# Two transformer-like blocks in one kernel: the memory's keys and values move into the MLP's last quarter, and the second block starts by token halves

## The reference, cut to what matters

```python
# end of the first block: an MLP of width 4096, then a norm over the features
h = rms_norm(x, g_mlp)
f = square(relu(h @ w_1))                       # 1024 -> 4096
x = x + f @ w_2                                 # 4096 -> 1024
x = rms_norm(x, g_final)

# second block (inputs with the suffix _2)
h = rmsnorm(x, norm_g)                          # norm of a norm: only factors per token
qk_raw, v, o, z_a, gates, u, z_b, qc, z_c = split(h @ w_in)
ig, fg = gates + b_gates                        # 4 heads each: they feed exponentials and cumulated sums over time
y_b = (pool(u) @ pool_w) * scale * silu(z_b)    # causal running means of 2, 4, 8, 16 tokens
km, vm = split(rmsnorm(mem, mem_norm_g) @ w_kv) # 256 memory rows, 4 heads
y_c = (softmax(q_c @ km.T / sqrt(128)) @ vm) * silu(z_c)
y_a = mlstm(qk_raw, v, o, ig, log_sigmoid(fg)) * silu(z_a)
x = x + concat(y_a, y_b, y_c) @ w_out           # y_b's part: blocks "ob"; y_c's: "oc"; y_a's: "oa"
out = rmsnorm(x, final_norm_g)
```

## Time and profile before

| | us |
|---|---|
| median of 3 runs | 2609.71 (2609.51 to 2610.11) |
| the profiled execution | 2607.73 |
| its span | 2605.9 |
| TensorE matmul busy | 2486.5 (95%) |
| VectorE busy | 1348.3 (52%) |
| ScalarE busy | 823.8 (32%) |
| mean granted TensorE clock | 0.982 |
| mean DMA rate | 54 GB/s |

### The profile page before, as it was taken

The page is one execution under the profiler, slowest core; times in us unless marked ns, Lnnn a source line. Parts: engine busy times, 40 slices in busy tenths (PEclk is TensorE's granted clock), DMA queues, the critical chain, the costliest instruction groups (busy, mean ns, idle before and its releaser), DMA issues.

```text
span 2605.9 us, 26395 instructions
## 1 busy us (share of the span) xinstructions
PE 2486.5 (95%) x11144; PEld 2011.0 (77%) x11144; DVE 1348.3 (52%) x1832; ACT 823.8 (32%) x1224; POOL 2.8 (0%) x7
## 2 busy tenths in 40 slices
PE   7999999999999999999999999998789999999678
PEld 6778677686786788888888888887678777878577
DVE  5588697897782724342232332334665333631365
ACT  5352432526113622331131220322422231221354
POOL 0000000000000000000000000000000000000000
PEclk9999999999999999999999999999899999999889
DMA  4102012021210112211111111121112111111401
GB/s 136 45 21 74 25 59 68 12 83 39 91 49 26 34 55 77 77 49 49 49 49 49 49 49 49 49 65 41 42 52 58 33 33 49 48 49 54 125 20 62
DMA packets 226680, 139.45 MB, mean 54 GB/s; under 512 B 12922, under 2 KB 221050, under 8 KB 226562
## 3 DMA queue, kind: packets, MB, share of 16 engines
q1 hardware_dynamic: 226562, 137.76, 17.9%
HBM read 128.27 MB, written 9.47 MB: 53 GB/s over the span
## 4 chain that ended last, share of the span: by engine, by line
PE 82%; DVE 11%; ACT 5%; issue 1%; DMA 1%; SPq 1%; DVEq 0%; ACTq 0%
PE bank L572 25%; PE bank L574 25%; PE bank L573 25%; PE bank L636 2%; PE bank L606 1%; DVE evens L1620 1%; DVE lru L1584 1%; DVE both L1633 1%; DVE odds L1627 1%; PE bank L821 1%; PE bank L837 1%; PE bank L729 1%; DVE wlo L1479 0%; DVE v L1558 0%; DVE lru L1574 0%
## 5 line engine op out<-in xcount | busy, mean ns | idle before, releaser
L572 PE MATMUL bank<-h_hi,whi 128*128 128x512 f32 x2000 | 788.1, 394 | 7.6 <-DVE wlo L1479 4.0
L574 PE MATMUL bank<-h_hi,wlo 128*128 128x512 f32 x2000 | 780.0, 390 | 0.0
L573 PE MATMUL bank<-h_lo,whi 128*128 128x512 f32 x2000 | 779.7, 390 | 0.0
L572 PEld LDWEIGHTS bank<-h_hi,whi 128*128 128x128 f32 x2000 | 376.5, 188 | 90.3 <-issue 11.3
L573 PEld LDWEIGHTS bank<-h_lo,whi 128*128 128x128 f32 x2000 | 376.5, 188 | 81.1 <-issue 3.6
L574 PEld LDWEIGHTS bank<-h_hi,wlo 128*128 128x128 f32 x2000 | 376.3, 188 | 79.1
L954 ACT ACTIVATE whi<-raw 128x1024 fp32r<-128x1024 f32 (+2 forms) x212 | 216.6, 1023 | 474.6 <-PE bank L574 469.3
L1479 DVE TENSOR_TENSOR wlo<-raw,whi 128x1024 fp32r<-128x1024 f32 (+2 forms) x212 | 251.1, 1185 | 208.9 <-ACT whi L954 207.4
L574 PE MATMUL bank<-ff_hi,wlo 128*128 128x512 f32 x512 | 199.2, 389 | 0.0
L572 PE MATMUL bank<-ff_hi,whi 128*128 128x512 f32 x512 | 199.2, 389 | 0.0
L573 PE MATMUL bank<-ff_lo,whi 128*128 128x512 f32 x512 | 199.2, 389 | 0.0
(11 more groups left out here) (354 smaller groups left out, 3142.7 us busy)
## 6 DMA issues: line engine op xcount, KB each, us to landing
raw<-in_w_in SPq DMA_DIRECT2D x92, 512.0 KB, 3.7
raw<-in_w SPq DMA_DIRECT2D x64, 512.0 KB, 3.8
raw<-in_w_b_out SPq DMA_DIRECT2D x16, 384.0 KB, 3.1
raw<-in_w_out SPq DMA_DIRECT2D x11, 512.0 KB, 3.5
x_in<-in_x SPq DMA_DIRECT2D x8, 512.0 KB, 5.6
raw<-in_w_a_out SPq DMA_DIRECT2D x8, 512.0 KB, 4.1
raw<-in_w_o SPq DMA_DIRECT2D x8, 512.0 KB, 3.6
xcols<-in_x SPq DMA_DIRECT2D x16, 256.0 KB, 2.8
```

The lines of the kernel that those rows point to most:

```text
L572: pe.matmul(target, lh, rh, start=start, stop=False, skip_group_check=True)
L573: pe.matmul(target, lh, rl, start=False, stop=False, skip_group_check=True)
L574: last = pe.matmul(target, ll, rh, start=False, stop=stop and point is not None, skip_group_check=True)
```

## The change

**The list of weights and TensorE's order.** Key blocks 0 and 1 go before `w2` block 5, and all other key and value blocks before `w2` block 6 of the last quarter. The memory is turned in two parts, behind `w2` blocks 2 and 3. Blocks 6 and 7 of `w2` come last, both first halves of tokens before the second ones. The token sums, the factors, their spreading and `h3` are made for each half of the tokens: the sums of the first half behind the first half of block 7 and the second half of block 6, its spread factors in the middle of block 7's second half. `gates` and `u` 0 run together, tile by tile of h3 (`tiles_together`), for the first half, with the sums of the second half in their middle; then the second half's factors, `u` 1's first half, `gates` and `u` 0 together for the second half, `u` 1's second half. Then `zb` and `pw` of group g with `u` of g+2 behind. The turn of `x_row` and the spreads `y1_scale` stand behind the last `pw`.

**DVE and ACT.** `x1`'s squares and sums go in halves of 512 tokens. `h3_low` subtracts one tile behind `h3_part`'s product. The row chain of the gates is cut: sums behind group 0, maxima (`gate_maxima`) behind the `ob` additions. The residual is scaled in front of the `ob` additions. In group g the steps of `pooled` for the next groups stand behind `yp_tile(g)`.

**SP.** The table `rcnt` is loaded with the memory. SP's wait for `m_row` stands behind the weight loads up to the second `qc` block, no longer behind those near the gates.

**Memory.** `row`, `tmp2` and `sqm` get other places.

```diff
--- before
+++ after
+        KV_AT = {5: (0, 1), 6: tuple(range(2, 2 * NH))}
...
             for j in range(DT):
                 need(("w1", f, j), w_1, 0, DT, (f * DT + j) * P, P)
             for j in range(DT):
+                if f == FC - 1:
+                    for c in KV_AT.get(j, ()):
+                        need_kv(c)
                 need(("w2", f, j), w_2, f * D, DT, j * P, P)
-        for c in range(NH):
-            need(("kv", c), w_kv, 0, DT, c * P, P)
...
+        for g in range(NH + 1):
+            if g < NH:
+                need(("u", g), w_in2, 0, DT, Y_U + g * P, P)
+            if g:
+                need(("zb", g - 1), w_in2, 0, DT, Y_ZB + (g - 1) * P, P)
+                need(("pw", g - 1), A["pool_w_2"][0, g - 1], 0, 1, 0, P)
...
+            sp.dma_start(rcnt[:], A["rcnt"]).then_inc(*landed("rcnt", ("rcnt",)))
...
-            ahead(number["gates"] + 2)
+            ahead(number["qc", 0] + 1)
             w.wait_ge(*at("m_row"))
...
+            def stat_sums(half):
+                w.wait_ge(*at("square_sums", DT - 1, half))
                 for n in range(2):
-                    for t in range(NT):
+                    for t in range(half * 4, half * 4 + 4):
                         last = pe.matmul(stat_bank[:, n * NT + t:n * NT + t + 1], square_sum[n][:, t * P:(t + 1) * P], ones[:, 0:1],
                                          start=True, stop=True, skip_group_check=True)
...
+                for j in range(DT if f < FC - 1 else DT - 2):
+                    if f == FC - 1:
+                        for c in KV_AT.get(j, ()):
+                            key_block(c)
+                    block(("w2", f, j), ff, f"ff{f}")
+                    if f == FC - 1 and j in (2, 3):
+                        turn_memory(4 * j - 8)
+                        turn_memory(4 * j - 6)
+            for c in range(2, NH):
+                key_block(c)
+            value_banks = [bank("values", q) for q in range(NM)]
+            for c in range(NH, 2 * NH):
+                value_block(c, value_banks)
+
+
+            for j in (DT - 2, DT - 1):
+                block_product(number["w2", FC - 1, j], ("w2", FC - 1, j, 0), ff, f"ff{FC - 1}", 0, used=False)
+            block_product(number["w2", FC - 1, DT - 2], ("w2", FC - 1, DT - 2, 1), ff, f"ff{FC - 1}", 1)
+            stat_sums(0)
+
+            def tiles_together(keys, half, right, right_name, middle=None):
+                together = [bank(*key, half) for key in keys]
+                for n in range(DT):
+                    if middle and n == 4:
+                        middle()
+                    w.wait_ge(*at(f"{right_name}_lo", n, half))
+                    for key, b in zip(keys, together):
+                        k = number[key]
+                        hi, lo = weight_views(k)
+                        w.wait_ge(*at("w", k))
+                        point = [(*key, half)] + ([("used", k)] if half else []) if n == DT - 1 else None
+                        three_products(b[:], (hi[:, n, :], lo[:, n, :]), (right[0][n][:, cut(half)], right[1][n][:, cut(half)]), n == 0,
+                                       point)
+
+            def factors(column, half, name):
+                w.wait_ge(*at("r12", half))
+                spread(column, half, name)
+
+            tiles_together([("w2", FC - 1, DT - 1)], 1, ff, f"ff{FC - 1}", lambda: factors(8, 0, "h3_scale"))
+
+
+            tiles_together([("gates",), ("u", 0)], 0, h3, "h3", lambda: stat_sums(1))
+            ring.names, ring.turn = ring.names + [("x1_var", 0), ("stat", 1)], 6
+            factors(8, 1, "h3_scale")
+            block_product(number["u", 1], ("u", 1, 0), h3, "h3", 0, used=False)
+            tiles_together([("gates",), ("u", 0)], 1, h3, "h3")
+            block_product(number["u", 1], ("u", 1, 1), h3, "h3", 1)
...
+            for g in range(NH):
+                block(("zb", g), h3, "h3")
+                pool_product(g)
+                if g + 2 < NH:
+                    block(("u", g + 2), h3, "h3")
+            b = bank("x_turn")
+            w.wait_ge(*at("x_row"))
+            for c in range(NT):
+                last = pe.transpose(b[:, c * NH:(c + 1) * NH], row[0][0:NH, c * P:(c + 1) * P], ident[0:NH, 0:NH])
+            last.then_inc(*up("pe_done", ("x_turned",)))
+            for half in range(2):
+                spread(0, half, "y1_scale")
...
+            columns = lambda n, half: slice(8 * n + 4 * half, 8 * n + 4 * half + 4)
+            for j in (DT - 2, DT - 1):
+                stat_square(j, 0)
+            root(columns(0, 0), "r1_0")
+            root(columns(1, 0), "r2_0")
+            ahead(number["w2", FC - 1, DT - 2] + 3)
+            stat_square(DT - 2, 1)
+            h3_part(0, 0, 1, 2)
+            stat_square(DT - 1, 1)
+            ahead(number["w2", FC - 1, DT - 1] + 3)
+            h3_part(0, 3, 4, 5)
+            root(columns(0, 1), "r1_1")
+            h3_part(0, 6)
+            root(columns(1, 1), "r2_1")
+            h3_part(0, 7)
...
+            gate_rows(0)
+            u_tile(0, 0)
+            h3_part(1, *range(DT))
+            gate_rows(1)
+            u_tile(0, 1)
+            ahead(number["zb", 0])
+            ahead(number["pw", 0])
+            split_pooled(0)
+            u_tile(1, 0)
+            u_tile(1, 1)
+            ahead(number["u", 2])
+            for g in range(NH):
+                zb_tile(g)
+                if g + 1 < NH:
+                    ahead(number["zb", g + 1])
+                split_yp(g)
+                if g < 2:
+                    split_pooled(g + 1)
+                    u_tile(g + 2, 0)
+                    u_tile(g + 2, 1)
+                ahead(number["u", g + 3] if g + 3 < NH else number["zb", NH - 1] if g == 1 else number["ob", min(g - 2, 1)])
+                if g == 0:
+                    act.activation(R(2), row[1][32:32 + NH, :], ACT.Copy).then_inc(*did(("f_row",)))
+                    w.wait_ge(*at("f_min"))
+                    act.activation(R(3), R(3), ACT.Exp).then_inc(*did(("f_exp",)))
+                    w.wait_ge(*now("act_done"))
+                    act.activation(R(3), R(3), ACT.Ln, bias=1.0).then_inc(*did(("f_ln",)))
+                if g == 1:
+                    split_pooled(3)
...
+            def square_sums(j, half):
+                total, weighted, sq_ = square_sum[0][:, cut(half)], square_sum[1][:, cut(half)], sqm[(2 * j + half) % 4]
+                w.wait_ge(*at("sqm", j, half))
                 own()
                 if j:
-                    dve.tensor_tensor(square_sum[0][:], square_sum[0][:], sqm[j % 2][:], ALU.add).then_inc(*did())
-                    dve.scalar_tensor_tensor(square_sum[1][:], sqm[j % 2][:], GF2[:, j, 1:2], square_sum[1][:], ALU.mult,
-                                             ALU.add).then_inc(*did(("square_sums", j)))
+                    dve.tensor_tensor(total, total, sq_[:], ALU.add).then_inc(*did())
+                    dve.scalar_tensor_tensor(weighted, sq_[:], GF2[:, j, 1:2], weighted, ALU.mult, ALU.add).then_inc(
+                        *did(("square_sums", j, half)))
...
+            for j in (DT - 2, DT - 1):
+                x2_tile(FC - 1, j, 0)
+                square_sums(j, 0)
+            w.wait_ge(*at("kv", 2 * NH - 1))
+            for n in range(3):
+                dve.memset(uw[n][:, 0:PAD_U], 0.0).then_inc(*did(*([("u_clear",)] if n == 2 else [])))
+            x2_tile(FC - 1, DT - 2, 1)
+            means(0)
+            second_means(0)
+            factors(0)
+            ahead(number["w2", FC - 1, DT - 2] + 3)
+            h3_part(0, 0, 1)
+            square_sums(DT - 2, 1)
+            h3_part(0, 2)
+            x2_tile(FC - 1, DT - 1, 1)
+            h3_low()
+            square_sums(DT - 1, 1)
+            ahead(number["w2", FC - 1, DT - 1] + 3)
+            h3_part(0, 3, 4, 5)
+            means(1)
+            h3_part(0, 6)
+            second_means(1)
+            h3_part(0, 7)
+            factors(1)
+            h3_low()
+            h3_part(1, *range(DT))
+            h3_low()
...
+            ahead(number["zb", 0])
+            ahead(number["pw", 0])
+            pooled(0)
+            ahead(number["u", 2])
+            for g in range(NH):
+                zb_tile(g)
+                if g + 1 < NH:
+                    ahead(number["zb", g + 1])
+                yp_tile(g)
+                if g < 2:
+                    pooled(g + 1)
+                ahead(number["u", g + 3] if g + 3 < NH else number["zb", NH - 1] if g == 1 else number["ob", min(g - 2, 1)])
+                if g == 0:
+                    gate_sums()
+                if g == 1:
+                    pooled(3)
+            w.wait_ge(*at("x_turned"))
+            dve.tensor_copy(xcol[:], bank("x_turn")[:, 0:NH * NT]).then_inc(*did(("xcol",), ("free", "x_turn")))
+            for half in range(2):
+                b = bank("y1_scale", half)
+                w.wait_ge(*at("y1_scale", half))
+                for j in range(DT):
```

(3 more changed lines are left out.)

404 lines of the change are left out of this document (193 added, 211 removed).

## The result

| | before | changed | 
|---|---|---|
| median of the runs | 2609.89 (2609.51 to 2610.11) | 2572.81 (2571.66 to 2573.80) |
| the profiled execution | 2607.73 | 2573.80 |
| its span | 2605.9 | 2571.8 |
| mean granted TensorE clock | 0.982 | 0.984 |

The changed kernel is faster: the ratio is 0.9858, with a 95% interval of 0.9841 to 0.9875. I had 2579.1 with 2571 to 2590.

The account below looks back on a forecast made before the run. TensorE, busy 95% of the span, bounds the kernel; only its waits and slow stretches count. 266.7 + 0.5 + 7.1 + 3.5 + 2.7 + 1.0 = 281.5 against 312.1, 30.6 less, gives 2579.1, range 2571 to 2590.

Parts of the forecast that it names:

- Work, 266.7: TensorE's work from 1715.9 to 2028.0, counted at the full clock: 266.7 us of a stretch of 312.1.
- The weight of `w2` 6, 0.5: Behind six short key and value blocks in a row, only this weight comes late, by 0.5 (bounds 0 and 4.4).
- The factors of the first half: DVE and ACT's 2.15 is covered by 2.7 of `w2` 7's second half; the wait of 3.9 goes.
- h3's first half, 7.1: Beside `gates` and `u` 0, TensorE waits for DVE's low parts: 7.1 in all, bounds 0 and 13.1.
- Low clock there, 3.5, and 1.0 behind `pw` 3: Clock falls once in h3's first half, costing 3.5 (bounds 0 and 9); 1.0 more behind the last pooling product's wait.
- The weight of `pw` 3, 2.7: Split behind pooled tile 3 and group 2's gating, it comes 2.7 late for TensorE (bounds 0 and 6).
- The rows, the pools and the scaling: Waits of 8.3 for `x_row` and 2.8 for `yp` go; 10.6 of residual scaling moves beside the `ob` products.
- The halves' cost on DVE, 2.2, not in the sum: Seven pairs of sums become fourteen: some 2.2 us of DVE beside `w2`, costing nothing there.
- The clock stays down: Rival: clock stays at 1.2 GHz from h3's first half until `u` 1 is done; 8.4 more, 2587.5; chance 0.14.
- DVE's queue is worse: Rival: ACT's hand-over in h3 is not hidden, each of eight tiles costs 0.75 more; 6.0, 2585.1; chance 0.14.
- Less is left: Rival: the clock does not fall and the weight of `pw` 3 is in time; 2571.9; chance 0.17.
- Slower: Rival: SP sits on `m_row` with later weights behind it, TensorE stands in `qc`; 2614 at 70 us; chance 0.03.

Follow-up runs that it names:

- eight-block kernel: Changed kernel with keys 0 and 1 moved behind `w2` 5, so that all eight short key and value blocks stand in one row; median 2575.5.
- sums behind `w2`: Changed kernel with TensorE asking for the first half's token sums and spread only behind the last product of `w2` 7; median 2576.3.
- the kernel with the wait filled: Changed kernel with twelve more matmuls of 512 columns on TensorE in front of h3's tile 3, first half; median 2570.0.
- the kernel with the rows part alone: Kernel before with only the turn of `x_row`, the `y1_scale` spreads and the residual scaling moved behind the last pooling product; median 2605.9.
- the kernel with the early scaling: Changed kernel with the `y1_scale` spreads and the 16 residual scalings again behind `u` 1, in front of the pools; median 2586.0.
- the kernel with the values last: Changed kernel with the four value blocks behind `w2` 7 and the second half's token sums directly behind them; median 2571.6.
- `u` 1 lags: Changed kernel with h3's tiles 0 to 5 made without a break and `u` 1's first five steps before the second half's token sums; median 2567.9.

## Why the prediction was right, and where it was off

The sum was 281.5 for a stretch that took 278.0, and the mechanism was the one forecast: the waits named went, and what is left stands where it was said to stand. That the sum came so near is in part luck: four terms were 5.8 too dear together, and the work and the clock in the gates block 2.3 too cheap. The median was missed by 6.3, 3.3 of it in the profiled execution and 3.0 in the offset from profile to median. Term by term:

- **Work, 266.7.** Held within 0.7.
- **The weight of `w2` 6, 0.5.** The profile shows no wait: the split ended at 1804.2 and the block began at 1804.35, at most 0.2 late. The eight-block kernel, with 1.0 of waits, shows that the rate was right and the place a bare fit.
- **The factors of the first half.** Nothing waits for them, as said; DVE needs 2.06 for them, 2.15 in the earlier trace rows. Asked for later, the kernel is slower, by 5.1 in the medians and 1.6 in the place itself (sums behind `w2`).
- **h3's first half, 7.1.** It was 4.5: 0.66, 0.97 and 2.82 for my 1.1, 1.1 and 3.4, at the tiles I named. The last two, 0.9 and 0.6 before tiles 5 and 6, did not come in this profile, since TensorE at the half clock was no faster than DVE; at full clock they are 0.2 and 0.3. This term was mis-sized by 2.6. The count of DVE's instructions between the tiles was right, and so was 1.3 a tile against the 2.05 of the earlier trace rows.
- **Low clock there, 3.5, and 1.0 behind `pw` 3.** In the profiled pair it is 5.1 in the first place and nothing in the second, 5.1 for my 4.5. But the step itself, that a wait of about 3 brings the clock down, did not hold as a rule: with the same wait the clock stayed in another execution, and the kernel with the wait filled won only about 1.5 by medians.
- **The weight of `pw` 3, 2.7.** It was 1.0, and it went when the split moved. The cause was right, the chain 1.7 shorter than I chained it.
- **The rows, the pools and the scaling.** `x_row`, `yp` and the gates' weight are no longer waited for. I priced the parts one by one, and that worked since I followed the new order; the kernel with the rows part alone shows that the same 8.3 is not a part's own: alone it is worth 2.7.
- **The halves' cost on DVE, 2.2, not in the sum.** I took 0.15 for each added instruction from durations, which overlap the next instruction. By starts in a dense row a whole addition takes 1.14 (1749.57 to 1750.71, before) and a half 0.61 (1833.68 to 1834.29): 0.08 more for two; the weighted ones 1.20 and 0.66, 0.12 more. That makes some 1.4 in all, between my two figures, and the trace does not show twice the 0.8 of the smaller one.
- **Outside the stretch, nothing.** Ahead of it the changed kernel took 1.3 less and behind it 1.2 more, in code that the change does not touch. The median gained 3 more than the profiled pair; my offset of 2.0 from profile to median, taken from before, was -1.0 for the changed kernel.

**What is not priced.** No run has the keys and values moved alone, or `gates` and `u` 0 run tile by tile alone. That these parts took away the waits of 8.8, 3.6 and 3.3 is read from the profile, where they are gone.

**The rivals.** "The clock stays down" had 19.0 of work at the half clock, 38.0 us long; it was 10.2 us in the profile. The Trainium skill (TensorE: Matmul & The Clock Gate, the section on a second HAM failure mode) has small idles between groups bring the clock down again and again. The traces agree in part: in both profiles of the changed kernel it fell once behind waits of 0.7, 1.0 and 2.8, for 10.2 us, and came back while the thin work went on; with the same waits in the kernel with the early scaling it did not fall at all. "DVE's queue is worse" is out: a tile costs 1.3. "Less is left" has the best time, 2571.9 against 2572.8, but only half its reasons: `pw` 3 was 1.0 late and not 2.7, and nothing fell behind it, but the clock did fall in the gates block in both profiles, and the shorter h3 waits are not of its making. That its time fits is luck. "Slower" did not come near: no new wait in the `qc` stage.

## What to carry to other kernels

A wait in an in-order queue is not worth its length but what is late right behind it: before pricing its removal, list the next two waits of the same engine, and do it with the new order, not the old. Where one engine is to feed another tile by tile, count what else stands between the tiles in its queue, and put weights, sums and other short jobs where it idles anyway; h3's products placed before the weight splits and not behind them, with the last pooling weight split earlier, were worth 5 us by medians, on the kernel with the values last. Compare clock effects by medians over runs: a single profile shows where the clock fell in that execution, and not that the kernel makes it fall.

## What the runs showed of the hardware

- The granted clock differs between executions of the same instructions. In code that all the kernels share, the profiles lose it at 840 (before: 0.91 from 840 to 860) or between 880 and 920 (changed: 0.91), and the first key product starts anywhere from 1770.1 to 1774.7.
- A fall to 1.2 GHz came behind waits of 0.2 and 0.4 in one profile (`u` 1 lags) and did not come behind one of 2.8 (scaling early). Behind the same wait of 2.8 it lasted 10.2 in two profiles (changed) and 3.4 in one (eight short blocks). What decides it is open; no run here tells it.
- Eight float32 matmuls of one column, which the trace lists as 16, take 1.70 at 2.4 GHz from the first start to the start of the next product (1820.79 to 1822.49). That is 0.21 each, nearly twice an fp32r matmul of 256 columns (0.120). Their busy time is 1.84, and 3.41 at 1.2 GHz.
